# Eight-head attention: inverting the row sums for two heads at once, in four pieces, with copies on ScalarE and products on GpSimd

## The reference, cut to what matters

```python
s = jnp.einsum('bqhd,bkhd->bhqk', qb, k).astype(jnp.float32) * scale
mask = cid[None, :] <= qc[:, None]
s = jnp.where(mask[None, None], s, neg)
p = jax.nn.softmax(s, axis=-1).astype(v.dtype)
return jnp.einsum('bhqk,bkhd->bqhd', p, v)
...
return o * jax.nn.silu(z)
```

## Time and profile before

| | |
|---|---|
| Median of three runs | 2271.89 us (2269.77 to 2271.94) |
| The profiled execution, its own time | 2269.03 us |
| Its span, first to last instruction | 2267.1 us |
| Mean granted TensorE clock | 0.956 of full speed |
| TensorE matmul busy | 2071.7 us (91%) |
| VectorE busy | 1079.5 us (48%) |
| ScalarE busy | 679.9 us (30%) |
| GpSimd busy | 378.3 us (17%) |
| First scores of head 0 to last values of head 7 | about 1935 to 2158 us |

### The profile page before, as it was taken

How to read it: one execution, slowest core, us unless ns; L and a number is a source line. 1 busy time by engine, 2 the same in 40 slices (tenths; PEclk the granted TensorE clock), 3 DMA queues, 4 the chain that set the end, 5 groups by cost and what they waited for, 6 DMA issues and landing times.

```text
span 2267.1 us, 24653 instructions
## 1 busy us (share of the span) xinstructions
PE 2071.7 (91%) x9965; PEld 1683.0 (74%) x9965; DVE 1079.5 (48%) x1700; ACT 679.9 (30%) x1171; POOL 378.3 (17%) x427
## 2 busy tenths in 40 slices
PE   7989799869999999999999999979899985888899
PEld 6767688757877888888888887759788873555577
DVE  5666635544454333333333355364544237666641
ACT  4544112145443121221221233341111136233321
POOL 3142203520020000000000022530422025000000
PEclk9989899969999999999999999989999988889999
DMA  4133232121111111111111120113111210000023
GB/s 136 38 110 104 88 87 75 45 80 56 43 51 47 48 46 56 47 47 47 47 47 56 47 65 27 47 50 118 32 29 40 57 44 4 0 1 0 28 75 93
DMA packets 175913, 122.29 MB, mean 54 GB/s; under 512 B 17785, under 2 KB 163449, under 8 KB 175801
## 3 DMA queue, kind: packets, MB, share of 16 engines
q1 hardware_dynamic: 175800, 120.73, 17.8%
HBM read 100.78 MB, written 19.92 MB: 53 GB/s over the span
## 4 chain that ended last, share of the span: by engine, by line
PE 76%; DVE 14%; ACT 4%; issue 2%; POOL 2%; DMA 1%; SPq 0%; ACTq 0%; DVEq 0%; POOLq 0%
PE ps L310 20%; PE ps L311 20%; PE ps L312 20%; PE ps L323 3%; PE ps L2556 3%; DVE rcp L2595 2%; PE ps L514 2%; PE ps L1171 1%; DVE wlo L297 1%; PE ps L2545 1%; DVE fm L907 1%; PE ps L1155 1%; PE ps L2546 1%; DVE xl L1435 1%; PE ps L2547 1%
## 5 line engine op out<-in xcount | busy, mean ns | idle before, releaser
L310 PE MATMUL ps<-xh,whi 128*128 128x512 f32 (+2 forms) x1728 | 694.1, 402 | 32.0 <-DVE wlo L297 18.5
L311 PE MATMUL ps<-xl,whi 128*128 128x512 f32 (+2 forms) x1728 | 674.1, 390 | 0.0
L312 PE MATMUL ps<-xh,wlo 128*128 128x512 f32 (+2 forms) x1728 | 670.7, 388 | 0.0
L310 PEld LDWEIGHTS ps<-xh,whi 128*128 128x128 f32 x1728 | 331.7, 192 | 108.1 <-issue 22.4
L312 PEld LDWEIGHTS ps<-xh,wlo 128*128 128x128 f32 x1728 | 330.6, 191 | 66.2
L311 PEld LDWEIGHTS ps<-xl,whi 128*128 128x128 f32 x1728 | 331.7, 192 | 62.0 <-issue 3.1
L291 ACT ACTIVATE whi<-wraw 128x1024 fp32r<-128x1024 f32 (+2 forms) x151 | 147.0, 973 | 363.8 <-PE ps L312 351.1
L297 DVE TENSOR_TENSOR wlo<-wraw,whi 128x1024 fp32r<-128x1024 f32 (+2 forms) x151 | 193.5, 1281 | 113.0 <-ACT whi L291 112.9
L310 PE MATMUL ps<-ffh,whi 128*128 128x512 f32 x512 | 199.4, 389 | 0.0
L311 PE MATMUL ps<-ffl,whi 128*128 128x512 f32 x512 | 199.3, 389 | 0.0
L312 PE MATMUL ps<-ffh,wlo 128*128 128x512 f32 x512 | 199.2, 389 | 0.0
(11 more groups left out here) (432 smaller groups left out, 2645.8 us busy)
## 6 DMA issues: line engine op xcount, KB each, us to landing
wraw<-w_in SPq DMA_DIRECT2D x47, 512.0 KB, 3.9
wraw<-w_up SPq DMA_DIRECT2D x32, 512.0 KB, 4.0
wraw<-w_down SPq DMA_DIRECT2D x32, 512.0 KB, 3.4
xt<-x SPq DMA_DIRECT2D x8, 512.0 KB, 7.1
wraw<-w_o SPq DMA_DIRECT2D x16, 256.0 KB, 2.9
xr<-x SPq DMA_DIRECT2D x8, 512.0 KB, 4.3
wraw<-w_ple_gate SPq DMA_DIRECT2D x8, 512.0 KB, 4.1
h_d<-hT SPq DMA_DIRECT2D x8, 512.0 KB, 3.5
```

The source lines that it names most:

```text
L310: pe.matmul(out, h, xh[:, k, c0:c1_], start=(k == 0), stop=False)
L311: pe.matmul(out, h, xl[:, k, c0:c1_], start=False, stop=False)
L312: mm = pe.matmul(out, l, xh[:, k, c0:c1_], start=False, stop=(k == nk - 1))
```

## The change

It does four things. (1) VectorE no longer reads the outputs and sums. ScalarE copies the sums of each half and head from PSUM to `den[hf]` and the outputs to `og[hf]` (64 partitions by 512 columns each), half 0 in unit 7 of the same head, half 1 in unit 2 of the next head, behind that unit's exponential. (2) VectorE inverts `den[hf]` once for a pair of heads, in place, over 128 partitions, in four pieces of 128 columns, one per unit: half 0 in units 10 to 13 of the odd head, half 1 in units 3 to 6 of the following even head; for the last pair the pieces of half 1 stand after the last unit. (3) GpSimd multiplies twice: `z` by `og`, then by the inverted `den`. The banks of outputs are given back by ScalarE's copy. (4) The 14 maxima products stand two to a unit in units 4 to 10, and the turn in unit 11, one unit earlier. `normed`, with its 16 reciprocals and 16 products, is gone.

```diff
--- before.py
+++ after.py
@@ -2436,7 +2436,9 @@
     pts = [X(f"pt{i}", 52480 + 2048 * i, [512]) for i in range(4)]
 
     aq, ak = X("aq", 16512, [T]), X("ak", 20672, [T2])
-    rcp = [M("rcp0", 92.25, [512]), M("rcp1", 100.125, [512])]
+
+    og = [X("og0", 60672, [512]), M("og1", 92.25, [512])]
+    den = [M("den0", 100.125, [512]), M("den1", 98, [512])]
     nmx = [M(f"nmx{i}", 102.25 + 0.09375 * i, [NB, 3]) for i in range(2)]
     nms = [M(f"nms{i}", 102.4375 + 0.40625 * i, [104]) for i in range(2)]
     AUG = 120
@@ -2454,7 +2456,7 @@
 
     chunks = [(i, c) for i in range(NB) for c in range((NMETA + 128 * (i + 1) + 511) // 512)]
     prepare = [[("kT", 0)], [("kT", 1)], [("kT", 2), ("qT", 0)], [("qT", 1)]] + [
-        [("max", m) for m in range(14 * n // 8, 14 * (n + 1) // 8)] for n in range(8)] + [[("turn", 0)], []]
+        [("max", 2 * n), ("max", 2 * n + 1)] for n in range(7)] + [[("turn", 0)], [], []]
     assert len(prepare) == nu and len(chunks) == 14
 
     def values_of(h, x):
@@ -2550,7 +2552,7 @@
             h, u = j // nu, j % nu
             hf, x, c0 = units[u]
             if x == 0:
-                take(w, "values", ("o", h, hf), (dve_at, ("o", h, hf)))
+                take(w, "values", ("o", h, hf), (act_at, ("o", h, hf)))
             w.wait_ge(*act_at.at("exp", h, u))
             w.wait_ge(*pool_la.at("ones"))
             pe.matmul(tile("o", h, hf)[:, c0:512], values_of(h, x), pts[j % 4][0:n_keys(x), 0:512 - c0], start=(x == 0), stop=(x == last_x[hf])
@@ -2569,6 +2571,15 @@
         values(8 * nu - 1)
 
     def attend_act(act, w):
+        def summed(h, hf):
+            a, b = 64 * (h % 2), 64 - 64 * (h % 2)
+            p = tile("o", h, hf)
+            w.wait_ge(*pe_at.at("values", nu * h + (4, nu - 1)[hf]))
+            if h > 1 and h % 2 == 0:
+                w.wait_ge(*pool_at.at("y", h // 2 - 1, hf))
+            act.activation(den[hf][a:a + 64, :], p[b:b + 64, :], ACT.Copy).then_inc(*act_at.up("den", h, hf))
+            act.activation(og[hf][a:a + 64, :], p[a:a + 64, :], ACT.Copy).then_inc(*act_at.up("o", h, hf))
+
         for h in range(-1, 8):
             for u in range(nu):
                 if h >= 0:
@@ -2578,41 +2589,43 @@
                     if j > 3:
                         w.wait_ge(*pe_at.at("values", j - 4))
                     act.activation(pts[j % 4][0:n_keys(x), 0:512 - c0], tile("unit", h, u)[0:n_keys(x), 0:512 - c0], ACT.Exp).then_inc(*act_at.up("exp", h, u))
+                    if u == 2 and h > 0:
+                        summed(h - 1, 1)
+                    if u == 7:
+                        summed(h, 0)
                 if h < 7:
                     for step in prepare[u]:
                         prepare_act(act, w, h + 1, *step)
+        summed(7, 1)
 
     def attend_dve(dve, w):
-        def normed(j):
-            h, u = j // nu, j % nu
-            hf, x, c0 = units[u]
-            if x == last_x[hf]:
-                a, b = 64 * (h % 2), 64 - 64 * (h % 2)
-                r, p = rcp[hf], tile("o", h, hf)
-                w.wait_ge(*pe_at.at("values", j))
-                if h > 1 and h % 2 == 0:
-                    w.wait_ge(*pool_at.at("y", h // 2 - 1, hf))
-                dve.reciprocal(r[a:a + 64, :], p[b:b + 64, :]).then_inc(*dve_at.up("rcp", h, hf))
-                w.wait_ge(*dve_at.at("rcp", h, hf))
-                dve.tensor_tensor(r[a:a + 64, :], p[a:a + 64, :], r[a:a + 64, :], ALU.mult).then_inc(*dve_at.up("o", h, hf))
+        def inverse(c, hf, n):
+            d = den[hf][:, 128 * n:128 * n + 128]
+            w.wait_ge(*act_at.at("den", 2 * c + 1, hf))
+            dve.reciprocal(d, d).then_inc(*dve_at.up("inverse", c, hf, n))
 
         for h in range(-1, 8):
             for u in range(nu):
-                if nu * h + u >= 2:
-                    normed(nu * h + u - 2)
                 if h < 7:
                     for step in prepare[u]:
                         prepare_dve(dve, w, h + 1, *step)
-        normed(8 * nu - 2)
-        normed(8 * nu - 1)
+                if h > 0 and h % 2 == 0 and 3 <= u < 7:
+                    inverse(h // 2 - 1, 1, u - 3)
+                if h > 0 and h % 2 == 1 and u >= 10:
+                    inverse(h // 2, 0, u - 10)
+        for n in range(4):
+            inverse(3, 1, n)
 
     def attend_pool(pool, w):
         for c in range(4):
             for hf in range(2):
                 z = zf2[:, c, 512 * hf:512 * hf + 512]
-                w.wait_ge(*dve_at.at("o", 2 * c + 1, hf))
+                w.wait_ge(*act_at.at("o", 2 * c + 1, hf))
                 w.wait_ge(*act_la.at("silu", c))
-                pool.tensor_tensor(z, z, rcp[hf][:], ALU.mult).then_inc(*pool_at.up("y", c, hf))
+                pool.tensor_tensor(z, z, og[hf][:], ALU.mult).then_inc(*pool_at.up("z o", c, hf))
+                w.wait_ge(*dve_at.at("inverse", c, hf, 3))
+                w.wait_ge(*pool_at.at("z o", c, hf))
+                pool.tensor_tensor(z, z, den[hf][:], ALU.mult).then_inc(*pool_at.up("y", c, hf))
 
 
 
```

## The result

The changed kernel takes 2219.82 us (median of 4 runs, 2216.88 to 2221.14), the one before 2271.91 (4 runs, 2269.77 to 2272.23): ratio 0.9771, 95% interval 0.9754 to 0.9788. That is 52 us less; the forecast was 2225, 47 less, and the result lies inside its range of 2214 to 2240. The profiled execution took 2216.88 us by its own time, 2214.8 by its span, against 2269.03 and 2267.1.

What follows compares the result with a forecast made beforehand. TensorE was taken to be bound by waits on VectorE and slow clock after them: 33 us idle plus 17 clock, less 4.5 new stalls and 0.4 at the end, saves 45.1; 2223.9 profiled, forecast 2225, range 2214 to 2240.

Steps and rivals of the forecast that it cites:

- The stalls: TensorE's waits for a maximum, `kl` and the shift go, 5.0 us a head, leaving 22.0 us at full clock.
- The clock: Slow TensorE clock after stalls in heads 0 to 5 goes: 17 us no longer lost.
- New stalls in heads 2, 4 and 6: Half 1's pieces in units 3 to 6 stand before six maxima and delay TensorE: 1.5 us a head, bounds 0 and 2.3.
- Head 0: From 30.4 us, 3.2 of idle time and 3.5 of clock lost after its stall go; 23.7 remains.
- The end: After the stage, the low parts start 0.4 us later; dense product 5.3 to 5.6 us after the last values.
- ScalarE: It gains 32 copies of 0.58 us, 19 in all; taken to cost 0, bounds 0 and 1.2 in seven heads.
- GpSimd: It gains 8 products of 1.33 us, awaited only by the next pair's ScalarE copy and the output stage.
- (a): Rival: the clock still dips to 1.2 GHz after new waits in the heads, costing 12 us: 2237; chance 0.12.
- (b): Rival: ScalarE's queue becomes the wait at unit 2 in 7 heads, with as many dips: 2245; chance 0.06.
- (d): Rival: GpSimd's products hold VectorE back, 1.3 us for each of 16, 21 us in all: 2246; chance 0.04.
- (e): Rival: no change, the time saved is lost in full to another wait of the next head; chance 0.02.
- (c): Rival: slower, as a piece costs nearly a whole reciprocal; 28 us per us over 0.98, up to 2291; chance 0.02.

Runs made afterwards that it cites:

- b_old_prep: The changed kernel with the maxima put back over units 4 to 11 and the turn in unit 12, as before; 2229.08 us.
- e_thrice: The changed kernel with every piece inverted three times in place, the value kept; 2274.69 us.
- f_split_only: The kernel before with each reciprocal from PSUM in four pieces of 64x128, one per unit, the product behind the last; 2233.59 us.
- c_whole: The changed kernel with each inversion in one piece of 128x512 where the first piece stood; 2241.21 us.
- a_prep_only: The kernel before with only the new placing: two maxima products a unit in units 4 to 10, the turn in unit 11; 2258.32 us.
- j_split_prep: f_split_only with the changed kernel's placing of maxima and turn added; 2232.93 us.

## Why the prediction was right, point by point

The sum can be held against the profiled execution: 2269.03 - 2216.88 = 52.2 us saved, 45.1 forecast. The 7 us lie in these terms:

- *The stalls*: right in kind. All three waits went, and heads 1, 3 and 5 take 21.49 us where the sum had 22.0: 1.5 us. The 22.0 were TensorE's busy time in a head with waits, with modelled ends. b_old_prep points the same way: a head lost 0.2 to 0.4 us more than its recorded idle time. The prediction kept this for the range's lower end and should have had it in the sum.
- *The clock*: right. By (1-c)T over heads 0 to 6, 20 us were lost before and 3.3 after, all of it in head 0: 17 us, as forecast.
- *New stalls in heads 2, 4 and 6*: mis-sized, 0.45 us a head and not 1.5. With the 0.5 above that is 23.5 forecast and 21.94 measured, 4.7 us over three heads, the largest miss. The step that failed counts four pieces before six maxima; in the program's order the fourth piece stands behind them, and the maxima of these units are short ones: 2.4 us busy for six, not 6 x 0.50. That leaves VectorE some 1.5 us less to do than the 7.6 reckoned. TensorE has more to do there than the 5.3 reckoned: units 3 to 6 of head 2 take 6.3 us from scores to scores, 5.9 without the waits.
- *Head 0*: 23.2 against 23.7. The slow start stayed (mean clock 0.86), the dip behind the stall went.
- *The end*: 4.8 us from the last values at 2105.9 to the dense product at 2110.72, 5.0 before, 5.4 in the sum and 5.3 to 5.6 among the signs of being right, which this misses: the recorded piece was right (0.925 against 0.95 us), but the next one starts 0.83 us after it.
- *ScalarE*: 0.592 us a copy against 0.58, and no wait of TensorE behind them, as taken. *GpSimd*: 1.27 us a product, the last one 1.60, against 1.33.

Of the rivals, (a), clock that still dips, did not happen: nothing in the changed kernel waits over 0.3 us between head 1 and head 7, and the clock stays at 1.00. (b), (d) and (e) did not either: `pt` and `qh` release TensorE nowhere new, and every piece took 0.89 to 0.95 us, also beside GpSimd's products. Where (d)'s rule of the Trainium skill does bite (SBUF - State Buffer, the section on who interferes with whom: two SBUF inputs against a reading GpSimd instruction), the trace agrees: of the first two low parts, 2.32 us together, the one that starts while the product runs took 1.77 us, where a low part alone takes 0.68, and the product 1.60 instead of 1.27. It was so before: 0.69 and 1.77, so the 1.19 each in (d) is a mean of two unlike ones. (c), slower through dear pieces, was imitated by e_thrice; its total was right to 3 us by luck, since its parts were not (above).

The fixed cost of a piece, for which the Trainium skill was cited (VectorE: DVE Perf Modes, the section on the TRN2 errata), can be seen in the recorded durations, 0.925 against 3.324/4 = 0.83 us, but hardly in VectorE's time: the next instruction starts 0.86 us after a piece begins among the maxima and 0.83 on average at the end. Nor does it depend on the source here: the pieces of f_split_only, read from PSUM, are recorded with 0.948 us. c_whole follows the rule's advice of at least 512 elements and is 21 us slower: where TensorE waits behind the instruction, its length weighs more than its fixed cost, and the measurement decides.

## What to carry to other kernels

Ask of an engine that is busy for half of a stage not how much it does but how long one instruction blocks what the bottleneck needs next: cutting the long instructions alone brought 38 of 52 us while the engine's work grew. What a second change is worth depends on the first: the earlier turn brought 13 us alone, 1 behind the pieces alone, and 9 with pairing, copies and later pieces in place. And read a recorded wait of TensorE as somewhat more lost time than it shows, plus what the clock loses after it.

## What the runs showed of the hardware that was not expected

- Four reciprocals of 128x128 with no wait between them took 3.39 us, about as much as one of 128x512 (3.324), though each is recorded with 0.89 to 0.95: the recorded durations of neighbours overlap, and adding them up overstates VectorE's time.
- The same wait was followed by 1.2 GHz in some heads and not in others. The `kl` waits of 1.7 to 1.8 us were in 3 of 6 heads before and in 4 of 6 in a_prep_only; the maximum waits of 2.6 to 2.7 in all but head 6 before, those of 2.2 to 2.5 in 3 of 7 in a_prep_only. None of the waits of 1.03 us in b_old_prep or of 1.5 to 1.6 in j_split_prep was: there the clock is 1.00 in heads 1 to 6.
- Taking out a wait of 0.6 us a head in a_prep_only went with 5 us less of slow clock, while both longer waits stayed, the one for maxima shorter by 0.3.
- Medians of the changed kernel in two sets of runs differed by 1.3 us, and 4.4 us between two kernels shrank to 1.9 when they were timed in one set; differences of this size need one set, or the length of the stage in the traces.
